# A hybrid decoder layer on eight cores: norm scales by Ln and Exp on ScalarE, transposes by DMA, and another order of loads

## The reference, cut to what matters

```python
h = rms_norm(x, norm_mix)                                  # x: [2048, 1024] on each core
q, k, v, u, g_a, g_p = split(h @ w_in)                     # 512, 512, 512, 512, 1024, 1024 columns
q = partial_rope(rms_norm(q per head, q_norm)); k = ...    # 8 heads of 64, rotary on 16 dims
o_attn = moba_attention(q, k, v)     # own block of 256 keys + the best 3 of the earlier blocks
o_pool = multiscale_pool(u)          # windows 2, 4, 8, 16, then a linear map per group
m = sigmoid(g_a) * (o_attn @ w_up_attn) + sigmoid(g_p) * (o_pool @ w_up_pool)
x = x + m @ w_out
x = x + square(relu(rms_norm(x, norm_mlp) @ w_ff1)) @ w_ff2   # 4096 wide
```

## Time and profile before

| | us |
|---|---|
| median of 3 runs (999.39 to 1002.57) | 999.39 |
| the profiled execution, its own time | 999.08 |
| its span, first to last instruction, slowest core | 997.8 |
| spans of the eight cores | 991.5 to 997.8 |
| TensorE busy | 934.3 (94%) |
| VectorE, ScalarE, GpSimd busy | 442.2, 362.3, 220.3 |

### The profile page before, as it was taken

One profiled execution on the slowest core, in us unless ns is written; L12 is line 12 of the kernel. 1 busy time (PEld: TensorE's weight loads), 2 busy tenths in 40 slices (PEclk: granted clock), 3 DMA queues, 4 the chain that ended last, 5 costly groups with the idle time before them and its releaser, 6 DMA issues.

```text
span 997.8 us, 16143 instructions; the slowest of 8 cores (991.5 to 997.8 us)
## 1 busy us (share of the span) xinstructions
PE 934.3 (94%) x5758; PEld 458.8 (46%) x5758; DVE 442.2 (44%) x741; ACT 362.3 (36%) x643; POOL 220.3 (22%) x327
## 2 busy tenths in 40 slices
PE   3478887999999989999999999999999999999998
PEld 1234445556655434444455444444444444444443
DVE  4546656656343212222376544444444344444443
ACT  2365667779987212222255411112110311111110
POOL 3678775363001243333300100000000000000000
PEclk8799999999999989999999999999999999999999
DMA  8942100027001992222290840343006600001113
GB/s 175 187 86 65 55 1 2 12 20 79 1 2 45 270 119 27 27 27 27 41 183 10 100 69 1 54 70 46 1 1 85 85 1 1 1 1 53 65 72 150
DMA packets 54844, 57.77 MB, mean 58 GB/s; under 512 B 22752, under 2 KB 45408, under 8 KB 54752
## 3 DMA queue, kind: packets, MB, share of 16 engines
q0 software_dynamic: 44400, 29.63, 23.5%
q1 hardware_dynamic: 9648, 26.24, 8.1%
q10 hardware_dynamic: 720, 0.89, 0.3%
HBM read 77.98 MB, written 8.39 MB: 87 GB/s over the span
## 4 chain that ended last, share of the span: by engine, by line
PE 83%; DMA 5%; POOL 5%; issue 4%; DVE 2%; ACT 1%; DVEq 0%; POOLq 0%; ACTq 0%
PE bank L546 50%; PE bank L1030 11%; PE bank L676 7%; DMA raw<-w_in 5%; PE bank L857 5%; PE bank L887 3%; PE bank L1040 3%; PE bank L1045 3%; POOL raw L698 2%; DVE raw L695 1%; PE bank L1124 1%; PE bank L732 1%; DVE raw L701 1%; POOL raw L536 1%; PE bank L931 0%
## 5 line engine op out<-in xcount | busy, mean ns | idle before, releaser
L546 PE MATMUL bank<-raw 128*128 128x512 bf16 x2304 | 500.1, 379 | 0.0
L546 PEld LDWEIGHTS bank<-raw 128*128 128x128 bf16 x2304 | 224.8, 98 | 268.1
L1156 ACT ACTIVATE raw<-bank 128x512 f32<-128x512 f32 x128 | 76.4, 597 | 337.2 <-PE bank L546 336.3
L1158 DVE SCALAR_TENSOR_TENSOR raw<-bank,raw 128x512 bf16<-128x512 f32 x128 | 88.5, 691 | 138.8 <-ACT raw L1156 138.8
L1174 DVE SCALAR_TENSOR_TENSOR raw<-bank,raw 128x512 f32<-128x512 f32 x128 | 96.1, 751 | 116.0 <-PE bank L546 116.0
L676 PE MATMUL bank<-raw 128*128 128x512 bf16 x512 | 134.0, 400 | 13.1 <-ACT raw L657 6.5
L865 ACT ACTIVATE raw<-bank 128x512 bf16<-128x512 f32 (+1 forms) x288 | 140.6, 598 | 15.0 <-PE bank L857 11.1
L1030 PE MATMUL bank<-raw 128*128 128x512 bf16 x512 | 118.8, 385 | 4.1 <-DMA raw<-w_in 4.1
L1051 DVE SCALAR_TENSOR_TENSOR raw<-raw,bank 128x512 f32<-128x512 f32 x64 | 44.0, 688 | 127.5 <-PE bank L1040 120.8
L857 PE MATMUL bank<-raw 128*128 128x512 bf16 (+1 forms) x320 | 91.8, 353 | 1.5 <-ACT raw L865 0.8
L887 PE MATMUL bank<-raw 128*128 128x65 bf16 x1088 | 77.4, 195 | 9.7 <-POOL raw L876 7.6
(11 more groups left out here) (88 smaller groups left out, 572.2 us busy)
## 6 DMA issues: line engine op xcount, KB each, us to landing
raw<-x SPq DMA_DIRECT2D x32, 512.0 KB, 9.9
raw<-w_ff POOLq DMA_DIRECT2D x16, 1024.0 KB, 17.0
out<-raw SPq DMA_DIRECT2D x32, 256.0 KB, 2.1
raw<-w_in POOLq DMA_DIRECT2D x8, 512.0 KB, 15.2
raw<-w_in POOLq DMA_DIRECT2D x16, 256.0 KB, 5.7
raw<-w_out POOLq DMA_DIRECT2D x2, 1024.0 KB, 30.8
raw<-w_up_attn POOLq DMA_DIRECT2D x8, 128.0 KB, 6.0
raw<-w_up_pool POOLq DMA_DIRECT2D x1, 1024.0 KB, 12.1
```

What stands on the lines that cost most here:

```text
L546: fns.append(lambda e, l=l, rr=rr, i=i: e.matmul(out_f(), lhsT=l(), rhs=rr(), start=(i == 0), stop=(i == len(pairs) - 1)))
L1156: op("act", c_act(512), lambda e, ps=ps, sq=sq: e.activation(out=sq.v, in_=ps.f, func=AF.Square), r=[ps], w=[sq], key=key + 1.73 * j)
L1158: op("dve", c_f32(512) + 0.05, lambda e, ps=ps, sq=sq, j=j: e.scalar_tensor_tensor(out=a1.v[:, j, :], in0=ps.f, scalar=0.0, in1=sq.v, op0= ...
```

## The change

- **Norm scales.** The power on GpSimd goes. In `x_chain` two ScalarE activations take its place (Ln with epsilon as bias, then Exp with scale -0.5), in `qk_tile` too. One table load at the start names a set with both functions, another is put ahead of the first Tanh of M.
- **Transposes.** `x_chain` of tiles 4 to 15 and all 16 tiles of O hand `hb` to a transposing DMA on SP's queue, which writes `hT`. The TensorE transposes and the bank copies of these 28 tiles go.
- **First loads.** The norm's gain is loaded as one row and spread over the partitions by two fp32 matmuls, no longer as 128 copies. Identity and mask are made on the chip. The small constants are one load. The rope table moves from ScalarE's queue to SP's. The warm-up matmuls read a zeroed tile and come in two lots.
- **Keys.** The copies into `kTe` and `kTo` write all 128 partitions, and two small DMAs per block on SP then put the 8 indicator rows over them. The zeroing and the two GpSimd loads go. (In `qz` the other head's rows stay zero.)
- **M and O.** The first eight units of M come in another order. `w_out` waits for slab 2 of M to be summed, the reload of `x` for slabs 3 to 6.
- **Keys of the scheduler.** Nine of its numbers and its rate for DMAs are new, so the first stage's order changes all over.

```diff
-DMA_BW = 0.33e6
+DMA_BW = 0.31e6
...
+PAR = dict(TP1=37.0, TP2=69.031, TP3=142.552, TA0=39.324, TA1=49.333, TA2=113.0, TA3=166.0, TM=242.0,
+           dtf=0.208, qoff=0.1, voff=0.5, u0=171.32, u1=250.937, goff=-7.086, xlead=0.589)
...
+        def dma_t(out, in_, r=(), w=(), key=0.0, after=()):
+            return g.op([("sp", 0.06, [lambda e: e.dma_start_transpose(out=out, in_=in_())])], r, w, key, "dmat", 0.35e6,
+                        "dmaT", after)
...
-        dma("act", bits_c, c_bits_d, 65536, w=[b_bits], key=-50)
+        dma("sp", gmix_r, gmix_d.rearrange("(a n) -> a n", a=1), 4096, w=[b_gmr], key=-51, seq="xload")
         load_x(0, -50)
+        dma("sp", small_c, c_small_d, 40960, w=[b_small], key=-48, seq="xload")
         load_w("k", -50)
-        dma("act", gmix, gmix_d.partition_broadcast(128), 0.1e6, w=[b_gmix], key=-49)
...
-            op("pool", 0.2, lambda e: e.tensor_scalar(
-                out=ss1[:, tt:tt + 1], in0=ss1[:, tt:tt + 1], scalar1=EPS, scalar2=None, op0=ALU.add),
-                r=[b_ss1[tt]], w=[b_ss1[tt]], key=key)
-            op("pool", 0.3, lambda e: e.tensor_tensor(
-                out=rstd1[:, tt:tt + 1], in0=ss1[:, tt:tt + 1], in1=mhalf[:, 0:1], op=ALU.pow),
-                r=[b_ss1[tt], b_mh], w=[b_rs1[tt]], key=key)
+            op("act", 0.2, lambda e: e.activation(
+                out=rstd1[:, tt:tt + 1], in_=ss1[:, tt:tt + 1], func=AF.Ln, bias=eps_c),
+                r=[b_ss1[tt], b_eps], w=[b_rs1[tt]], key=key)
+            op("act", 0.12, lambda e: e.activation(
+                out=rstd1[:, tt:tt + 1], in_=rstd1[:, tt:tt + 1], func=AF.Exp, scale=-0.5),
+                r=[b_rs1[tt]], w=[b_rs1[tt]], key=key)
...
+            if tt >= 4:
+                dma_t(hT[:, :, tt * 128:(tt + 1) * 128], lambda: hb.v, r=[hb], w=[b_hT[tt]], key=key)
+                return
...
-            op("pool", 0.5, lambda e: e.tensor_tensor(out=msb[mi], in0=msa[mi], in1=mhalf[:, 0:8], op=ALU.pow),
-               r=[b_msa[mi], b_mh], w=[b_msb[mi]], key=key)
+            op("act", 0.12, lambda e: e.activation(out=msb[mi], in_=msa[mi], func=AF.Ln),
+               r=[b_msa[mi]], w=[b_msb[mi]], key=key)
+            lnops.append(op("act", 0.12, lambda e: e.activation(out=msb[mi], in_=msb[mi], func=AF.Exp, scale=-0.5),
+                            r=[b_msb[mi]], w=[b_msb[mi]], key=key))
...
+            if n == "k":
+                for dst, bb, p0 in ((kTe, b_kTe[blk], 64), (kTo, b_kTo[blk], 0)):
+                    dma("sp", dst[p0:p0 + 8, :, blk * 256:(blk + 1) * 256],
...
-        m_order = [(f, G) for f in range(2) for G in range(3)] + [(0, 3), (1, 3)]
+        m_order = [(0, 0), (0, 1), (0, 2), (1, 0), (0, 3), (1, 1), (1, 2), (1, 3)]
...
-                w=[b_wo[hf]], key=TO - 60, after=r2_bufs + z_bufs)
+                w=[b_wo[hf]], key=TO - 60, after=r2_bufs + z_bufs + b_mT[2])
...
-                after=r2_bufs + [b_ropq, b_ropk] + ([tmp] if tt in (13, 14) else []))
+                after=r2_bufs + [b_ropq, b_ropk] + b_mT[3 + tt // 4] + ([tmp] if tt in (13, 14) else []))
...
-            ps = pF.tile("h2")
-            op("pe", 0.0565 * 8, [lambda e, c=c, hb=hb, ps=ps: e.transpose(
+            dma_t(hT[:, :, tt * 128:(tt + 1) * 128], lambda hb=hb: hb.v, r=[hb], w=[b_h2[tt]], key=ko + 0.5, after=b_hT)
```

More of the change, by code:

```diff
@@ L319, in run @@
             if trace is not None:
-                trace.append((e, st, self.free[e], o.tag, o.key, o.end))
+                trace.append((e, st, self.free[e], o.tag, o.key, o.end, len(alt[2]), o.dma))
             for t in o.tiles:
@@ L607, in build_nc @@
         dma("sp", band.bitcast(F32), c_band_d, 0.28e6, w=[b_band], key=70, seq="xload")
-        op("pool", 0.2, lambda e: e.memset(mhalf, -0.5), w=[b_mh], key=-60)
+        op("dve", 0.1, lambda e: e.memset(eps_c, EPS), w=[b_eps], key=-60)
+        op("act", 1.5, [lambda e: e.preload_act_table_set("natural_log_exp_and_others"),
+                        lambda e: e.activation(out=rden[0][:, 0:1], in_=eps_c, func=AF.Ln)], r=[b_eps], w=[Buf("d")], key=-70)
+        op("dve", 0.1, lambda e: e.memset(ident, 1.0), w=[b_bits], key=-60)
+        op("dve", 0.1, lambda e: e.memset(tri01, 1.0), w=[b_tri], key=-60)
+        op("dve", 0.1, lambda e: e.memset(ones_f, 1.0), w=[b_onf], key=-60)
+        op("pool", 0.3, lambda e: e.affine_select(
+            out=ident, in_=ident, pattern=[[1, 128]], compare_op=ALU.is_equal, fill=0.0, base=0, channel_multiplier=-1),
+            r=[b_bits], w=[b_bits], key=-45, after=b_w["k"])
+        op("pool", 0.3, lambda e: e.affine_select(
+            out=tri01, in_=tri01, pattern=[[1, 128]], compare_op=ALU.is_ge, fill=0.0, base=0, channel_multiplier=-1),
+            r=[b_tri], w=[b_tri], key=0)
+        for hf in range(2):
+            pg_ = pF.tile("gm")
+            op("pe", 0.9, lambda e, hf=hf, pg_=pg_: e.matmul(
+                pg_.f, lhsT=ones_f, rhs=gmix_r[:, hf * 512:(hf + 1) * 512], start=True, stop=True),
+                r=[b_onf, b_gmr], w=[pg_], key=-60)
+            flex(c_act(512), lambda e, hf=hf, pg_=pg_: e.activation(
+                out=gmix[:, hf * 512:(hf + 1) * 512], in_=pg_.f, func=AF.Copy),
+                c_f32(512), lambda e, hf=hf, pg_=pg_: e.tensor_copy(out=gmix[:, hf * 512:(hf + 1) * 512], in_=pg_.f),
+                r=[pg_], w=[b_gmix], key=-60)
         op("dve", 0.1, lambda e: e.memset(ones_b, 1.0), w=[b_ones], key=-60)
         op("dve", 0.3, lambda e: e.memset(vA[:, :, :, 64:65], 1.0), w=[b_vo], key=-20)
-        for pr in range(4):
-            op("dve", 1.1, lambda e, pr=pr: e.memset(kTe[64:128, pr, :].bitcast(F32), 0.0), w=[b_kpe], key=5)
-            op("dve", 1.1, lambda e, pr=pr: e.memset(kTo[0:64, pr, :].bitcast(F32), 0.0), w=[b_kpo], key=5)
         for s in range(2):
@@ L619, in build_nc @@
                    w=[b_qp[s]], key=10)
-        for i in range(2):
-            dst = kTe[64:72] if i == 0 else kTo[0:8]
-            b_ = b_kpe if i == 0 else b_kpo
-            dma("pool", dst, c_ind_d.rearrange("p (a b) -> p a b", a=4), 0.26e6, r=[], w=[b_], key=6)
         for rp, o0, bb in ((rope_k, 32, b_ropk), (rope_q, 0, b_ropq)):
@@ L670, in build_nc @@
         ms_i = [0]
+        lnops = []
         toks = {}
@@ L1034, in build_nc @@
                         seq="mg" if half == 0 else None)
-                op("act", c_act(512), lambda e, tm=tm, ps=ps: e.activation(
-                    out=tm.v, in_=ps.f, func=AF.Tanh, scale=0.5), r=[ps], w=[tm], key=km)
+                ft = mi == 0 and gi == 0
+                op("act", c_act(512) + (1.3 if ft else 0), ([lambda e: e.preload_act_table_set("exp_and_others")] if ft else [])
+                   + [lambda e, tm=tm, ps=ps: e.activation(out=tm.v, in_=ps.f, func=AF.Tanh, scale=0.5)],
+                   r=[ps] + ([] if ft else [b_tab]), w=[tm] + ([b_tab] if ft else []), key=km)
             for gi in range(2):
@@ L1220, in _host_consts @@
         band[:, 1024 + g * 16:1024 + (g + 1) * 16] = np.where((tp - 128) > (tq - w), 1.0 / w, 0.0)[:, 0:16]
-    return rope, band, np.eye(128, dtype=np.float32), (tq >= tp).astype(np.float32)
+    return rope, band
 def _bf16_bits(a):
@@ L1236 @@
     x = f(x)
-    rope, band, ident, tri = _host_consts()
+    rope, band = _host_consts()
     gq, gk = f(q_norm)[0], f(k_norm)[0]
-    small = np.zeros((128, 16), dtype=np.float32)
+    small = np.zeros((128, 80), dtype=np.float32)
     for col, gg in ((0, gq), (1, gk)):
@@ L1252 @@
         "gmix": f(norm_mix)[0], "gmlp": f(norm_mlp)[0],
-        "c_bits": np.concatenate([_bf16_bits(ident), _bf16_bits(tri)], axis=1),
-        "c_small": small, "c_gv": gv, "c_rope": rope, "c_band": _bf16_bits(band),
-        "c_ind": np.ascontiguousarray(np.broadcast_to(ind[:, None, :], (8, 4, S)).reshape(8, 4 * S)),
+        "c_small": small, "c_rope": rope, "c_band": _bf16_bits(band),
+        "c_ind": _bf16_bits(np.broadcast_to(ind[:, None, :], (8, 4, S)).reshape(8, 4 * S)),
     }
```

109 lines of the change are left out of this document (52 added, 57 removed).

## The result

| | us |
|---|---|
| median before (4 runs beside the changed kernel, 999.39 to 1002.57) | 999.85 |
| median after (4 runs, 941.48 to 958.48) | 941.79 |
| ratio, 95% interval | 0.9413, 0.9391 to 0.9435 |
| profiled execution, its span (slowest core) | 941.63, 940.6 |

The account below looks back on a forecast made before the run. DMA was taken to bound the first 49.1 us and TensorE's work O and FF, with second-stage idle time mostly waits for GpSimd. 6 + 4 + 13 + 7.2 + 7.0 = 37.2 us off 999.08 gave 962, range 944 to 973.

Parts of the forecast that it names:

- Powers: Second stage: Ln and Exp on ScalarE remove two thirds of TensorE's 19.1 us of waits for GpSimd, 13 us.
- First loads: First stretch: weights land about 4 us earlier and up to 16 more matmuls run before them; 6 us, between 2 and 8.
- Transposes in the first stage: First stage: 96 TensorE matmuls go, worth 5.4 us of its work; 4 us taken, between 1 and 5.4.
- M: Stage M: the third slab's late weights no longer delay units, slow clock included; 7.2 us, between 4.1 and 7.2.
- O: Stage O: 16 tiles lose 0.45 us of TensorE transposes each, 7.0 us, with no loss at a 5.7 us landing.
- the formula 4 x (L - 2.6) - 13.8: Stage O: time lost when transposing DMAs land after L us, VectorE falling behind beyond TensorE's 13.8 us of banks.
- the first pair: Stage O: landing of the first pair of transposes is hidden by 14 residuals that stand ahead of the second.
- the sign of being wrong: Transposing DMAs: a median landing above 8 us would be one of the signs that the forecast is wrong.
- B: Second stage: Ln and Exp wait behind exponentials on ScalarE, none of the 13 us comes; 975 us, chance 0.20.
- C: Stage O: transposes land late, 6 to 13 us; at 9.9 us O loses 15.4 us, giving 977; chance 0.10.
- D: Stage O: transposes land so late, past 15.3 us, that the kernel is slower, above 999 us; chance 0.06.
- E: ScalarE: Ln and Exp pairs change the function table each time, 96 loads of 1.28 us; about 1050 us, chance 0.02.

Follow-up runs that it names:

- b_ln: Kernel before with Ln and Exp on ScalarE in place of all GpSimd powers, scheduler free: 974.7 us, ratio to before 0.976.
- r_pow: Changed kernel in its kept instruction order with all powers back on GpSimd: 969.8 us, ratio to before 0.972.
- a_gmix: Changed kernel with the first norm's gain loaded as 128 copies on ScalarE's queue again, scheduler free: 944.5 us, ratio to before 0.946.
- a_m: Changed kernel with M's old unit order and the old conditions for `w_out` and the reload of `x`, scheduler free: 945.2 us, ratio to before 0.946.
- r_t2o: Changed kernel in its kept order with every transposing DMA of O done twice, the second waiting for the first: 985.6 us, ratio to before 0.985.
- b_lnxt: Kernel before with Ln and Exp for the powers and transposing DMAs for x tiles 4 to 15: 972.9 us, ratio to before 0.971.
- a_par: Changed kernel with the old scheduler numbers and DMA rate, scheduler free: 946.8 us, ratio to before 0.951.

## Why the prediction was wrong, point by point

**Powers: the step that failed.** "Of the 19.1 us of waits for GpSimd I take two thirds, 13 us." Done alone (b_ln) the step is worth 21.7 us in its stage; undone alone, in the kept order (r_pow), 28. The mechanism was right, the term was too small, by two things. First, the two thirds: nearly all waits for GpSimd went, 19.1 to 2.5 in b_ln and to 4.6 in the changed kernel, and idle time fell by 16.4. The discount was for new waits of a Ln behind VectorE's sum; ScalarE waits 4.4 us for it over the whole run (L723 above), and TensorE hardly feels that. Second, only idle time was priced. The slow clock behind a wait has its own price: the same matmuls took 5.3 us less in b_ln and 9.3 more in r_pow. The prediction had both numbers at hand: it read 0.66 in the earlier trace rows, and in M it booked 7.2 us for 4.1 us of idle time with "slow clock behind it included". Here it left this out, in the upper bound of the range too, which was the stage's idle time of 27.3 us.

**First loads: 6 forecast, 7.8 measured on the slowest cores, 6.3 in the mean of the eight.** The size was right, but not for all of the reasons given. The extra matmuls ahead of the last weights, up to 3.4 us in the forecast, did not come: 32 matmuls of projections stand ahead of the wait before and after, and TensorE's next 24 begin at 41.31, after a wait of 5.54 us for `w_in`. The weights themselves landed earlier than forecast, by 6 us instead of 4. Of the parts of the new loads only the gain's was tried alone (a_gmix, 1.4 us in the mean of the cores); what the others give stays open.

**Transposes in the first stage: 4 forecast, 4.8 alone (2.7 of it in the stage) and 3.6 on top of Ln and Exp.** The size was about right there. That undoing it in the changed kernel costs 14 to 18 shows that parts under one scheduler do not add up, not that the step is worth that much.

**M: 7.2 forecast, 7.1 measured** between the slowest cores, and no new wait. That the two agree is partly luck, since both are read from one core: TensorE's waits for `w_in` in M of the kernel before are 4.1 us on that core and 1.3 to 4.2 on the eight. a_m got only 3.4 back, with a wait of 2.5.

**O: 7.0 forecast, 6.7 measured** for O and FF together. The median landing of 11.6 us, at which the formula 4 x (L - 2.6) - 13.8 would give a loss of 22, is not that of the steps it counts. It comes of four landings, 14.3 of the first pair, which the forecast called hidden, and three in FF. Fillings in O itself waited 0.2 to 1.3 us for their transposes and went on 3.1 to 4.6 us after these were issued, so landing was quicker there than the 5.7 of the forecast, and the formula too gives no loss. The long wait, 8.27 us at 513 us, stands in FF, where TensorE has other work for long:

```profile
513.35 1.22 DVE L1154 TENSOR_TENSOR raw<-raw 128x1024 bf16<-128x1024 f32 x1 [8.27 <-DMA raw<-raw]
```

So the sign of being wrong, a median above 8 us, came without a loss: one landing time for all steps says too little. The formula's idea, VectorE falling behind until TensorE's banks are full, is what r_t2o shows, with more than the formula's 26 to 28 us.

**The sum.** Of the second stage's 35.7 us, 21.7 are Ln and Exp (b_ln), 3.6 the transposes on top of it (b_lnxt), 1.8 the scheduler's numbers (a_par, M's start in the mean of the cores). Some 9 us are not assigned. The wider copies of the keys, the indicator rows and the zeroing that went were not tried alone, nor was the order that comes of all parts together.

**The rivals.** B, the wait moving to ScalarE, fell: ScalarE waits 4.4 us for VectorE's sums, and TensorE 1.3 us for ScalarE in that stage. C and D, late transposes, fell: TensorE never waits for one, nor, in O and FF, for work that stands behind one. In a_par it does on one core of eight, for 3.4 us, so the margin is small. E fell: two table loads, 1.28 us each. The Trainium skill, "ScalarE: Activation LUTs", section "Table sets: the hidden batching unit", has one set with both ln and exp; the trace agrees, with no third load. The Trainium skill, "DMA: Bandwidth & Descriptors", section "Latency and other measured facts", gave 261 GB/s, by which a transposing DMA of 262 KB would take an estimated 1.0 us. The trace differs: it has 3.1 us from issue to landing at best and 20.4 at most, and the measurement decides.

## What to carry to other kernels

Price a wait of TensorE with the slow clock behind it, not by its idle time alone: here one us of idle time cost 1.3 to 1.8 us (21.7 for 16.4 in b_ln, 28.1 for 18.8 in r_pow, 7.2 for 4.1 in M). Before discounting a removed wait for "what comes late next", name that next waiter and bound it; if the row says 0.2 us an instruction, the discount has to be small. In a kernel whose order comes from a scheduler, do a part alone in the kernel before and undo it in the kernel after: where the two differ (5 and 17 here), neither is the price of the part, and an undoing in the kept order has to tell what the new order cost. And look at all cores before pricing a wait: on the slowest one it can be the longest of eight.
